# Prompt attention: value products in two half-precision parts, every second weighting on GpSimd

## The reference

```python
def shared_attention(qg, qpos, k, v, kpos, mask, slopes):
    s = einsum('btkgd,bnkd->bkgtn', qg, k) * HD ** -0.5
    s = s - slopes[...] * (qpos[:, None] - kpos[None, :])
    p = masked_softmax(s, mask)
    return einsum('bkgtn,bnkd->btkgd', p, v), p

# prompt, for a block of 128 queries, 8 heads in 2 groups that share keys and values:
o = g[..., 0:1] * o_cmp + g[..., 1:2] * o_slc + g[..., 2:3] * o_win
```

## Time and profile before

| | us |
|---|---|
| median of 3 runs | 2917.19 (2915.94 to 2918.55) |
| the profiled execution | 2923.37 |
| its span, first to last instruction | 2921.7 |
| busy in the span: TensorE | 2741.7 (94%) |
| VectorE | 1270.4 (43%) |
| ScalarE | 1150.8 (39%) |
| GpSimd | 352.8 (12%) |

### The profile page before, as it was taken

How to read it: one execution, slowest core, us unless ns; L and a number is a source line. 1 busy time by engine, 2 the same in 40 slices (tenths; PEclk the granted TensorE clock), 3 DMA queues, 4 the chain that set the end, 5 groups by cost and what they waited for, 6 DMA issues and landing times.

```text
span 2921.7 us, 47262 instructions
## 1 busy us (share of the span) xinstructions
PE 2741.7 (94%) x18103; PEld 1823.3 (62%) x18103; DVE 1270.4 (43%) x2097; ACT 1150.8 (39%) x1593; POOL 352.8 (12%) x530
## 2 busy tenths in 40 slices
PE   5888898997999998999999999899998999999997
PEld 3667666655555564666666666566665666666664
DVE  8254454324555636444444122532336444443123
ACT  4664654322666724444444111211124444443111
POOL 0320303323000000111111000011100111111000
PEclk9899999999999999999999999999999999999999
DMA  3222223363000031111111111111111111111111
GB/s 131 79 73 63 67 64 121 105 187 110 1 1 1 4 112 37 51 50 50 50 50 53 64 49 41 44 50 50 51 44 37 52 49 49 50 50 64 53 54 59
DMA packets 113483, 173.19 MB, mean 59 GB/s; under 512 B 16993, under 2 KB 83922, under 8 KB 112978
## 3 DMA queue, kind: packets, MB, share of 16 engines
q1 hardware_dynamic: 92610, 150.90, 16.1%
q0 software_dynamic: 3792, 12.58, 1.3%
q10 hardware_dynamic: 16960, 8.16, 1.0%
HBM read 161.47 MB, written 14.30 MB: 60 GB/s over the span
## 4 chain that ended last, share of the span: by engine, by line
PE 78%; DVE 8%; SPq 6%; ACT 4%; issue 3%; DMA 1%; ACTq 0%; DVEq 0%
PE PS L1726 61%; PE PS L2050 5%; PE PS L2064 2%; ACT xT L823 2%; SPq L534 2%; SPq L537 2%; DVE R L1184 2%; PE PS L1706 2%; PE PS L1759 1%; PE PS L2021 1%; PE PS L1827 1%; DVE hT L1189 1%; PE PS L2022 1%; SPq L464 1%; SPq L459 1%
## 5 line engine op out<-in xcount | busy, mean ns | idle before, releaser
L1726 PE MATMUL PS<-hT,R 128*128 128x344 f16 x10152 | 1487.3, 310 | 6.1 <-DVE R L510 4.9
L1726 PEld LDWEIGHTS PS<-hT,R 128*128 128x128 f16 x10152 | 992.4, 98 | 498.4 <-DVE R L510 3.3
L510 DVE SCALAR_TENSOR_TENSOR R<-W,R 128x1024 f16<-128x1024 f32 (+1 forms) x186 | 248.5, 1336 | 964.2 <-ACT R L504 963.7
L504 ACT ACTIVATE R<-W 128x1024 f16<-128x1024 f32 (+1 forms) x186 | 206.5, 1110 | 923.6 <-PE PS L1726 919.3
L1726 PE MATMUL PS<-R 128*128 128x344 f16 x3276 | 478.2, 309 | 0.0
L1726 PEld LDWEIGHTS PS<-R 128*128 128x128 f16 x3276 | 320.2, 98 | 157.6
L1622 DVE SCALAR_TENSOR_TENSOR R<-R 128x1024 f32<-128x1024 f32 x96 | 123.3, 1285 | 79.3 <-ACT R L1127 78.0
L2050 PE MATMUL PS<-R 128*64 128x256 f32 (+1 forms) x592 | 155.0, 391 | 1.1 <-ACT R L1023 0.9
L823 ACT ACTIVATE xT<-xT 64x1024 f32<-64x1024 f32 x64 | 124.8, 1950 | 57.2 <-DMA xT<-cmp_t 56.0
L723 POOL COPY R<-R 128x2 f32 x88 | 19.4, 220 | 1035.8 <-ACT R L1126 1035.8
L1624 DVE SCALAR_TENSOR_TENSOR R<-R 128x1024 f32<-128x1024 f32 x96 | 123.3, 1285 | 13.6 <-DVE R L1623 12.3
(11 more groups left out here) (290 smaller groups left out, 2551.7 us busy)
## 6 DMA issues: line engine op xcount, KB each, us to landing
W<-wk SPq DMA_DIRECT2D x154, 512.0 KB, 3.4
W<-wdn SPq DMA_DIRECT2D x32, 704.0 KB, 4.0
xT<-cmp_t SPq DMA_DIRECT2D x256, 64.0 KB, 1.9
xT<-x SPq DMA_DIRECT2D x16, 516.0 KB, 7.3
o_y<-hT SPq DMA_DIRECT2D x6, 688.0 KB, 3.5
o_win_s<-state_win POOLq DMA_DIRECT2D x1, 4088.0 KB, 24.0
R<-s_hgrn POOLq DMA_DIRECT2D x4, 512.0 KB, 5.5
o_hgrn_s<-R ACTq DMA_DIRECT2D x4, 512.0 KB, 3.2
```

Source lines behind the costliest of these rows:

```text
L504: act.activation(to[:, n, 0, 0:width], W[:, n, 0:width], ACT.Copy, scale=UNIT).then_inc(wh_here, 1)
L510: dve.scalar_tensor_tensor(to[:, n, 1, 0:width], W[:, n, 0:width], UNIT, to[:, n, 0, 0:width], ALU.mult, ALU.subtract).then_inc(w_split, 1)
L1726: ins = pe.matmul(wide(u)[:, m, :], weights[half], src[:, other, m * TW:(m + 1) * TW], start=(first and half == other == 0), stop=(last an ...
```

## The change

- The values of the selected and the window branch (VP) and the compressed one (VPC) are split once into half-precision parts, high by ScalarE and low by VectorE, which stand beside each other in one 128-column stationary block for each of the two groups of heads. This stands in the single tokens' attention, ahead of the queries' parts on ScalarE and behind them on VectorE.
- The turned weights are scaled by 1024 and split too: ScalarE writes the high part (L1023's new form), then VectorE reads the same PSUM bank again and writes the low part (`low_part`); only that frees the bank and lets the product go.
- A product of a block is two half-precision matmuls, 128x128 stationary and 128x256 moving, one with the high and one with the low weights. Bank 6 then holds the part of the high values in 64 rows and that of the low values in the other 64. ScalarE copies the second to OTHER (`heads_out`), VectorE adds both into `mix` (`heads_sum`).
- The three multiplications of `weighted` for every even unit go to GpSimd; VectorE keeps reciprocal and gate. GpSimd's splits of `mix` move from ahead of the loop to behind the weighting of units 28, 36, 44 and 52.
- VectorE's order becomes: heads_sum(m-1), biased(2m+3), the small half of weighted(2m+2), then low_part for each group, and at group number groups/2 biased(2m+4) ahead of it and weighted(2m+3) behind it.

```diff
-        PT = reg(23992, 4, 4 * P)
+        PRODUCT = 1024.0
+        OTHER = reg(26608, 2 * P)
...
+        PT = halves(reg(23992, 2048)).rearrange("p (t s n) -> p t s n", t=4, s=2)
+        VP = halves(reg(10320, 2048)).rearrange("p (c t g n) -> p c t g n", c=2, t=NC, g=2)
+        VPC = halves(reg(28736, P)).rearrange("p (g n) -> p g n", g=2)
...
         SCORES, TURNED = 6, 4
+
+        def by_pool(n):
+
+            return n % 2 == 0
+
+        def weigh_turn(n):
+
+            return sum(by_pool(k) == by_pool(n) for k in range(n))
...
             wait_full(pool, U_S + 7)
-            for k in range(HA):
+
+            def mix_parts(k):
                 pool.tensor_copy(H2[:, k, 0, :], mix[:, k, :]).then_inc(mix_hi, 1)
                 pool.wait_ge(mix_hi, k + 1)
                 pool.tensor_tensor(H2[:, k, 1, :], mix[:, k, :], H2[:, k, 0, :], ALU.subtract).then_inc(mix_a, 1)
+
+            for n in range(len(units)):
+                i = units[n][0]
+                if by_pool(n):
+                    pool.wait_ge(rg_here, n + 1)
+                    for c, cols in spans(i):
+                        part = SS[n % SCORES][:, cols]
+                        ins = pool.tensor_scalar(part, part, RG[:, n % SCORES, c:c + 1], None, ALU.mult)
+                    ins.then_inc(pw_pool, 1)
+                if n in (28, 36, 44, 52):
+                    mix_parts((n - 28) // 8)
...
+            act.wait_ge(kl_here, 12)
+            for g in range(2):
+                part = slice(64 * g, 64 * g + 64)
+                for c, values in enumerate((VSL, VWN)):
+                    act.activation(VP[:, c, :, g, part], values[:, :, part], ACT.Copy).then_inc(vh_here, 1)
+                act.activation(VPC[0:NCP, g, part], VCP[0:NCP, part], ACT.Copy).then_inc(vh_here, 1)
             wait_full(act, U_S + 6)
...
             def heads_out(m):
                 i, j, half = units[2 * m]
                 rows = slice(64 * half, 64 * half + 64)
+                other = slice(64 - 64 * half, 128 - 64 * half)
                 act.wait_ge(pv_full, m + 1)
-                act.activation(mix[rows, HA + j:HA + j + 2, i * P:(i + 1) * P],
-                               PS[rows, 6, 0:2 * P].rearrange("p (a b) -> p a b", b=P), ACT.Copy).then_inc(pv_free, 1)
+                act.activation(OTHER[rows], PS[other, 6, 0:2 * P], ACT.Copy, scale=1 / PRODUCT).then_inc(oth_here, 1)
...
-                    act.activation(PT[:, turn % TURNED, 0:cols], PS[:, TURN_BANKS[turn % 3], 0:cols], ACT.Copy
-                                   ).then_inc(t_free, 1)
+                    act.activation(PT[:, turn % TURNED, 0, 0:cols], PS[:, TURN_BANKS[turn % 3], 0:cols], ACT.Copy,
+                                   scale=PRODUCT).then_inc(th_here, 1)
...
+                    dve.wait_ge(vh_here, 6)
+                    for g in range(2):
+                        part, to = slice(64 * g, 64 * g + 64), slice(64 - 64 * g, 128 - 64 * g)
+                        for c, values in enumerate((VSL, VWN)):
+                            dve.tensor_tensor(VP[:, c, :, g, to], values[:, :, part], VP[:, c, :, g, part], ALU.subtract
+                                              ).then_inc(vl_here, 1)
+                        dve.tensor_tensor(VPC[0:NCP, g, to], VCP[0:NCP, part], VPC[0:NCP, g, part], ALU.subtract
+                                          ).then_inc(vl_here, 1)
             wait_full(dve, U_S + 7)
...
+            def heads_sum(m):
+
+                i, j, half = units[2 * m]
+                rows = slice(64 * half, 64 * half + 64)
+                dve.wait_ge(oth_here, m + 1)
+                dve.scalar_tensor_tensor(mix[rows, HA + j:HA + j + 2, i * P:(i + 1) * P],
+                                         PS[rows, 6, 0:2 * P].rearrange("p (a b) -> p a b", b=P), 1 / PRODUCT,
+                                         OTHER[rows].rearrange("p (a b) -> p a b", b=P), ALU.mult, ALU.add).then_inc(pv_free, 1)
+
+            def low_part(m, g):
+
+                i = units[2 * m][0]
+                turn = group_at[m] + g
+                cols = 2 * P * len(blocks(i)[2 * g:2 * g + 2])
+                dve.wait_ge(th_here, turn + 1)
+                dve.scalar_tensor_tensor(PT[:, turn % TURNED, 1, 0:cols], PS[:, TURN_BANKS[turn % 3], 0:cols], PRODUCT,
+                                         PT[:, turn % TURNED, 0, 0:cols], ALU.mult, ALU.subtract).then_inc(t_free, 1)
...
                     dve.tensor_tensor(rg[:, 1:3], rg[:, 1:3], gate[:, 1:3], ALU.mult).then_inc(rg_here, 1)
                 else:
                     dve.tensor_tensor(rg, rg, gate, ALU.mult).then_inc(rg_here, 1)
+                if by_pool(n):
+                    return
                 dve.wait_ge(rg_here, n + 1)
                 for c, cols in spans(i):
                     part = SS[n % SCORES][:, cols]
@@ -1512,10 +1576,18 @@
...
             for m in range(len(units) // 2):
+                if m:
+                    heads_sum(m - 1)
                 biased(2 * m + 3)
                 weighted(2 * m + 2)
-                biased(2 * m + 4)
-                weighted(2 * m + 3)
+                count = groups[units[2 * m][0]]
+                for g in range(count):
+                    if g == count // 2:
+                        biased(2 * m + 4)
+                    low_part(m, g)
+                    if g == count // 2:
+                        weighted(2 * m + 3)
+            heads_sum(len(units) // 2 - 1)
             dve.wait_ge(pv_full, len(units) // 2)
             dve.wait_ge(nat_out, 16 * 6)
             dve.wait_ge(snat_out, 16 * 6)
...
                 def values(g):
                     turn = group_at[m] + g
                     pe.wait_ge(t_free, turn + 1)
                     if g == 0 and m:
                         pe.wait_ge(pv_free, m)
+                    if g == m == 0:
+                        pe.wait_ge(vl_here, 6)
                     for b, (kind, t, _) in enumerate(bl[2 * g:2 * g + 2]):
-                        p = PT[:, turn % TURNED, 2 * b * P:2 * (b + 1) * P]
+                        high, low = (PT[:, turn % TURNED, n, 2 * b * P:2 * (b + 1) * P] for n in range(2))
                         if kind == "cmp":
-                            v, p = VCP[0:NCP, rows], p[0:NCP]
+                            v, high, low = VPC[0:NCP, half, :], high[0:NCP], low[0:NCP]
                         else:
-                            v = (VSL if kind == "slc" else VWN)[:, t, rows]
-                        ins = pe.matmul(PS[rows, 6, 0:2 * P], v, p, start=(g == b == 0), stop=(2 * g + b == len(bl) - 1),
-                                        skip_group_check=True)
+                            v = VP[:, ("slc", "win").index(kind), t, half, :]
+                        out = PS[:, 6, 0:2 * P]
+                        pe.matmul(out, v, high, start=(g == b == 0), stop=False, skip_group_check=True)
+                        ins = pe.matmul(out, v, low, start=False, stop=(2 * g + b == len(bl) - 1), skip_group_check=True)
                     return ins
 
-                pe.wait_ge(pw_here, 2 * m + 2)
+                for n in (2 * m, 2 * m + 1):
+                    pe.wait_ge(pw_pool if by_pool(n) else pw_here, weigh_turn(n) + 1)
                 for g in range(groups[i]):
```

More of the change, by code:

```diff
@@ L310, in program @@
         kl_here = sem("kl_here")
+        vh_here = sem("vh_here")
+        vl_here = sem("vl_here")
+        th_here = sem("th_here")
+        oth_here = sem("oth_here")
+        pw_pool = sem("pw_pool")
         qh_here = sem("qh_here")
@@ L2036, in second @@
                 bl = blocks(i)
-                rows = slice(64 * half, 64 * half + 64)
                 def values(g):
```

## The result

The changed kernel takes 2939.99 us (median of four runs, 2937.38 to 2946.28) against 2917.27 us before (four runs by now); the ratio is 1.0079, 95% interval 1.0064 to 1.0094. It is slower by 22.7 us, where the prediction had 18.6 (2936). The profiled execution took 2946.28 us, with a span of 2944.5.

A forecast was written before the change was run, and what follows sets the result against it. TensorE paces the stage before, VectorE's chain with its waits after. Chain 300.9 - 2.8 + 2.5 + 4 - 5.2 = 299.4 us for 280.8: +18.6, median 2936 us; forecast 2926 to 2951, whole range 2914 to 2956.

The forecast's parts named there:

- The pair of i=7: A pair of units of the last row block takes 14.4 us where it took 13.7.
- The low part: VectorE's second PSUM read per group: 0.713 us for 512 columns (0.69 to 0.75), 102.6 us with narrow ones.
- The rival of a cheap low part: 16-bit operand and result double VectorE's rate: 0.45 us a wide low_part, 2903 us, turning at 0.56 us; chance 0.08.
- Small steps behind one another: VectorE's short steps in a pair: reciprocal and gate together 0.40 us to the next start, a biased 1.85 us.
- The middle wait: For i of 4 to 7 VectorE waits for scores standing behind group 0's products: 7.6 us in 15 pairs.
- The wait between pairs: After the last low part VectorE waits for TensorE's last products and scores: 49.6 us in 31 gaps, including heads_sum.
- GpSimd: Its weighting costs 1.6 to 3.4 us for a unit of 1599 columns and stays hidden.
- the rival did not come true: GpSimd holds VectorE: above 3.3 ns a column, full weightings wait, 30 to 60 us more, 2966 to 2996; chance 0.07.
- The splits of mix: Behind four units' weighting on GpSimd, together 4 to 6 us, they hold VectorE's weighting: +4 us (0 to 9).
- The start: With the splits gone from the stage's start, the first pair ends at 741.1 instead of 746.3 us: -5.2 us.
- The clock: TensorE's granted clock stays 1.00; by the rival it falls to 0.50, +56 us, 2992 us; chance 0.06.
- Edits at nothing: Building the values' parts costs nothing: VectorE's low ones, 3.2 us, fit its 5.79 us idle time before 713.24 us.

The follow-up runs named there:

- both hoists and the splits ahead: Changed kernel with scores issued earlier on TensorE, mid-pair and between pairs, and GpSimd's splits of mix ahead of the loop: 2882.37 us, ratio 0.9873.
- the filler version: Changed kernel with extra half-precision matmuls, whose result nobody reads, in TensorE's idle times of a pair: 2941.82 us, ratio 1.0077.
- the splits-ahead version: Changed kernel with GpSimd's four splits of mix back ahead of the loop: 2930.61 us, ratio 1.0041.
- the version with the middle hoist: Changed kernel, splits of mix ahead of the loop, only the scores of unit 2m+4 moved ahead of group 0's products: 2904.50 us, ratio 0.9958.

## Why the prediction was right, and where its terms were off

**What bounds the stage: right, and shown.** VectorE's chain and its two waits replaced TensorE as the pace. Less work on VectorE shortens the stage by as much (73.6 us for 74.4), more work lengthens it (37.3 for 30.8); taking the waits out by order turns +0.8% into −1.5% with every operation of the change in place. VectorE was busy 256 us up to 1045 us, near the 267 of the prediction. TensorE was busy 236, not near 205, since its matmuls last longer at the lower clock: 221 us in the 31 pairs at 0.93, 203 with both hoists and the splits ahead at 0.98.

**The pair of i=7** was put at 14.4 us; the three after the first took 14.54, 13.53 and 14.40. The spread is the clock: in the filler version, at 1.00 over these pairs, they took 13.75, 13.53 and 13.22. So at the clock that I had assumed the walk was 0.9 us too long, most of it by the next two points less the third; nearness to 14.4 is the lower clock's doing.

**The low part** (0.713 us for 512 columns, ends 0.69 and 0.75): a single one takes 684 ns, but what follows without a wait starts after 0.60 us (three in 1.88 us at 854.16). The group row:

```profile
L1546 DVE SCALAR_TENSOR_TENSOR R<-PS,R 128x512 f16<-128x512 f32 x136 | 88.5, 684 | 4.8 <-ACT R L1059 4.7
```

The term was 0.10 too large, for 129 of them 13 us. The 0.03 us for a wait, added from the eight copies of the earlier trace rows, isn't there: a wait that is already satisfied left no gap. The rival of a cheap low part had the right direction, and 0.60 in effect is not far from its turning point of 0.56: with this term alone put right, the forecast would have been about +6 us.

**Small steps behind one another.** From the reciprocal (853.87) to the low part (854.16) 0.29 us pass, where I took 0.40 to the next start, and each of the two biased lasts 1.77 us, not 1.85. In the i=5 pair some 0.3 us went so, about 9 us in 31 pairs. I worked this out from one pair; it wasn't tested by itself.

**The middle wait** (7.6 us in 15 pairs): 14.1 in the splits-ahead version, 17.2 in the changed kernel, by the idle times before the second biased. Two steps failed. Group 0's products take 0.64 us, not 0.44: its second block is the compressed one, and before and behind its matmuls on 63 rows the next start is 0.20 us away, not 0.11 (so 0.32 us for each of the two blocks: 854.90, 855.22, 855.54). And cheaper low parts hide less. Both make 0.43 us a pair, 6.5 us in 15 pairs. The 3 us more in the changed kernel are three waits of 1.97 to 2.26 us, with a granted clock of 0.57 to 0.71 in the 3 us before each.

**The wait between pairs** (49.6 us with 14 for heads_sum, so 36): the rows of the version with the middle hoist give 30.0 for ScalarE's copy and 7.5 for scores, 37.5. In the pair above it is 1.96 us from the last low part to the next biased, as walked. Right. (The prediction reads 1.37 us from 773.33 to 774.67 where the rows give 1.34; up to VectorE's start at 774.90 its sum is the same.)

**GpSimd** (1.6 to 3.4 us a unit, dear end for a two-input operation): 5.77 us for a unit of i=7 (1024+640+63 columns, 721.50 below), 4.50 for i=5 (854.34), outside the bounds. At i=7, where it meets VectorE's multiplications, that is the 3.3 ns a column from which the rival was to decide; by the shape rows of the last section, 5.2 us, it is 3.0. The prediction named over 3.5 us as a sign that it is wrong, yet the rival did not come true, because VectorE reaches its own multiplications 5.4 us after GpSimd starts in that pair (854.34 to 859.78), some of it thanks to the middle wait. It can hold VectorE: in the splits-ahead version at the stage's start three multiplications that met GpSimd's 1024-column one took 2.69 us instead of 1.38:

```profile
721.50 5.77 POOL L740 TENSOR_SCALAR R<-R 128x1024 f32<-128x1024 f32 x3
...
723.10 2.69 DVE L1570 TENSOR_SCALAR R<-R 128x1024 f32<-128x1024 f32 x3
```

Low parts are not held: three take 1.88 us beside GpSimd's weighting (854.16 and 854.34), and their mean is 644 ns with it and 640 where GpSimd does nothing (all weighting on VectorE). That agrees with the Trainium skill (GPSIMD Engine Reference, section 1, Specifications), which names VectorE's instructions in a two-port mode or with two SBUF inputs as the ones that contend: low_part has one of its two inputs in PSUM.

**The splits of mix** (+4 us, 0 to 9): about 16 in the profiled stage. The failed step follows from the last: weighting and split together last 7.4 us (901.81 to 909.2), not 4 to 6, so the split's second operation falls right on VectorE's weighting. And a hold of 2 us there was counted once, while TensorE's idle time, the lower clock after it and a late next pair add as much again.

**The start** (−5.2 us): the first pair's copy came at 744.6 us instead of 746.34, −1.7. The stage itself began 1.05 us later: its first biased starts at 717.75 us, before the change at 716.70, and over the profiles of all versions anywhere from 709.2 to 717.8, so that 1 us tells nothing of the change. The rest fell to the clock, 0.69 from 720 to 725 us, where the second biased waited for its scores (before, then after):

```profile
720.55 1.22 DVE L1483 CUSTOM_DVE_ANT_0 R<-PS,R 128x1024 f32<-128x1024 f32 x1 [1.74 <-PE PS L2022]
...
723.02 1.23 DVE L1527 CUSTOM_DVE_ANT_0 R<-PS,R 128x1024 f32<-128x1024 f32 x1 [3.16 <-PE PS L2094]
```

From the first biased to the first copy it is 29.6 us before and 26.8 after. In the filler version, where the clock is 1.00 up to 725 us, it is 24.6, and the gain is 5.0: as walked.

**The clock** (1.00 forecast, rival 2992 us): 0.93 in the stage. Taking for each of the 31 pairs the shortest of three kernels that differ only in splits and filler gives 286.5 us. The changed kernel's 306.9 are 20.4 more; 16.8 of them lie in the nine pairs at and behind the splits, 3.6 in others, most of it the three long middle waits. So the rival's premise held in part (the clock falls, in short stretches) at a small part of its price. The Trainium skill (TensorE: Matmul & The Clock Gate, A second HAM failure mode: psum-queue depth-cycling) warned of it, and the stage's mean of 0.93 against 1.00 before agrees more than the rows that I had set against it.

**Edits at nothing.** VectorE builds the values' low halves from 708.53 to 711.3 us, and 3.00 us of its idle time are left behind them: hidden, as said.

Together: −13 (low part), −9 (small steps, from one pair), +6.5 (middle wait), +13 (splits), +4 (clock elsewhere), +3.5 (start) on 18.6 make about 24, and the profiled stage ends 24.3 us later than before (1051.5 against 1027.17). The forecast was near because errors of −22 and +27 us met: its mechanism stands on the experiments, its nearness in the number was luck.

## What to carry to other kernels

Relief of the engine that paces is worth only what the next chain leaves, so walk that chain with its waits: here VectorE was 78% busy and still set the stage. When two engines hand work to and fro, put what the other one needs next ahead of work that only you need; the same reorder gave nothing where one engine was full and 48 us where none was. And before moving side work into another engine's gaps, add up both jobs' durations there, from a row of that very form of operation.

## What the runs showed of the hardware that I had not expected

- GpSimd's multiplication by a factor per partition costs about 2.5 ns a column and 0.3 us fixed (1024 columns in 2844 ns, 63 in 470), more than its subtraction of two tensors (1032 in 2148) and almost three times its conversion (1032 in 1043); group rows by shape:

```profile
L738 POOL TENSOR_SCALAR R<-R 128x63 f32<-128x63 f32 x22 | 10.3, 470 | 0.0
...
L730 POOL TENSOR_TENSOR hT<-R,hT 128x1032 f16<-128x1032 f32 x4 | 8.6, 2148 | 0.3
L738 POOL TENSOR_SCALAR R<-R 128x1024 f32<-128x1024 f32 x3 | 8.5, 2844 | 62.1 <-DVE R L1564 62.1
...
L728 POOL CAST hT<-R 128x1032 f16<-128x1032 f32 x4 | 4.2, 1043 | 0.0
```

- TensorE's granted clock fell to 0.66 in stretches of 5 us (750 to 755, 805 to 810) though TensorE's longest waits around them were 1.8 and 1.6 us, and 12% more matmul work did not change the stage's mean. What sets it there stays open.
